# A table set that holds both ln and exp, loaded by hand ahead of the root pairs of a two-block transformer kernel

## The reference, cut to what matters

```python
def rmsnorm(t, g):
    y = t32 * lax.rsqrt(jnp.mean(t32 * t32, axis=-1, keepdims=True) + EPS)
# first block, per layer: q, k, v, gates, ... = (rmsnorm(x) * (1 + sc1) + sh1) @ w_in
#   mLSTM over chunks of 128 tokens in both directions; its gates use log_sigmoid
#   mlstm_post: h * rsqrt(mean(h * h) + EPS) per head, times sigmoid(o)
#   conv branch and gated branch, each with a layernorm; then @ w_out; x = x + g1 * ...
#   x = x + g2 * swiglu(rmsnorm(x) * (1 + sc2) + sh2)
# after both layers: rmsnorm(x, final_g)
# second block, layer 0: dilated window attention; layer 1: grouped window attention
#   x = layer_norm(ALPHA * x + h); x = x + sigmoid(x @ w_ple_gate) * (p @ w_ple_proj)
```

## Time and profile before

| | |
|---|---|
| Time, median of 3 runs | 2807.26 us (2797.67 to 2810.21) |
| The profiled execution: its time | 2797.02 us |
| The profiled execution: its span | 2795.2 us |
| Mean granted TensorE clock | 0.97 of full speed |
| HBM traffic | 86 GB/s over the span |

### The profile page before, as it was taken

How to read it: one execution, slowest core, us unless ns; L and a number is a source line. 1 busy time by engine, 2 the same in 40 slices (tenths; PEclk the granted TensorE clock), 3 DMA queues, 4 the chain that set the end, 5 groups by cost and what they waited for, 6 DMA issues and landing times.

```text
span 2795.2 us, 39634 instructions
## 1 busy us (share of the span) xinstructions
PE 2653.1 (95%) x14364; PEld 2196.1 (79%) x14364; DVE 1439.5 (51%) x2110; ACT 777.0 (28%) x1591; POOL 1614.2 (58%) x1684
## 2 busy tenths in 40 slices
PE   7799998999999997999889999899999999889998
PEld 7688887888888886788767878677888888667876
DVE  6894354564464665915543333533444444555754
ACT  3322353211121114134421111312222222233423
POOL 6343224376576664534467777676666666655464
PEclk9898999899999999999999999999999999999999
DMA  7211015133233322211123222333323333223231
GB/s 311 98 54 38 31 31 203 62 124 123 70 137 102 112 90 60 67 53 53 54 75 92 96 90 94 103 113 96 93 90 92 98 99 91 83 67 88 79 98 61
DMA packets 79406, 256.59 MB, mean 92 GB/s; under 512 B 9888, under 2 KB 13728, under 8 KB 78880
## 3 DMA queue, kind: packets, MB, share of 16 engines
q1 hardware_dynamic: 61424, 211.64, 23.3%
q10 hardware_dynamic: 17840, 43.03, 4.8%
HBM read 237.33 MB, written 2.10 MB: 86 GB/s over the span
## 4 chain that ended last, share of the span: by engine, by line
PE 44%; POOL 28%; issue 19%; DVE 5%; ACT 2%; POOLq 1%; DMA 1%; SPq 0%; ACTq 0%; DVEq 0%
POOL w_lo L421 16%; POOL w_hi L419 10%; PE PS L427 8%; PE PS L430 8%; PE PS L428 8%; PE PS L1518 4%; PE PS L1519 4%; PE PS L1520 4%; POOL word L414 2%; PE PS L1383 1%; PE PS L1401 1%; DVE Z L2208 1%; PE PS L1505 1%; DVE AC L2290 1%; DVE XL L2215 1%
## 5 line engine op out<-in xcount | busy, mean ns | idle before, releaser
L421 POOL TENSOR_TENSOR w_lo<-raw,w_hi 128x512 fp32r<-128x512 f32 (+1 forms) x662 | 951.4, 1437 | 55.3
L427 PE MATMUL PS<-XH,w_hi 128*128 128x512 f32 x2168 | 824.8, 380 | 35.0 <-DVE XL L2565 7.9
L428 PE MATMUL PS<-XL,w_hi 128*128 128x512 f32 x2168 | 796.7, 375 | 0.0
L430 PE MATMUL PS<-XH,w_lo 128*128 128x512 f32 x2168 | 747.5, 376 | 0.0
L414 POOL TENSOR_TENSOR word<-ones 128x1 f32<-128x1 f32 x331 | 93.7, 283 | 1089.1 <-PE PS L430 736.2
L419 POOL TENSOR_SCALAR w_hi<-raw 128x512 fp32r<-128x512 f32 (+1 forms) x662 | 541.7, 818 | 0.0
L427 PEld LDWEIGHTS PS<-XH,w_hi 128*128 128x128 f32 x2168 | 412.7, 190 | 144.6 <-issue 25.6
L428 PEld LDWEIGHTS PS<-XL,w_hi 128*128 128x128 f32 x2168 | 412.8, 190 | 75.6
L430 PEld LDWEIGHTS PS<-XH,w_lo 128*128 128x128 f32 x2168 | 382.6, 190 | 60.3
L1518 PE MATMUL PS<-XH,w_hi 128*128 128x512 f32 (+1 forms) x640 | 236.5, 369 | 16.0 <-DVE XL L2215 16.0
L1519 PE MATMUL PS<-XL,w_hi 128*128 128x512 f32 (+1 forms) x640 | 230.2, 360 | 0.0
(11 more groups left out here) (326 smaller groups left out, 3479.3 us busy)
## 6 DMA issues: line engine op xcount, KB each, us to landing
raw<-in_wgu SPq DMA_DIRECT2D x88, 512.0 KB, 3.5
raw<-in_wa SPq DMA_DIRECT2D x80, 512.0 KB, 3.6
raw<-in_win SPq DMA_DIRECT2D x48, 512.0 KB, 3.5
modv<-in_wmod ACTq DMA_DIRECT2D x48, 512.0 KB, 5.2
raw<-in_wdn SPq DMA_DIRECT2D x32, 512.0 KB, 3.5
QS<-Z ACTq DMA_DIRECT2D x100, 128.0 KB, 3.5
modt<-in_wmod SPq DMA_DIRECT2D x20, 512.0 KB, 15.0
raw<-in_wout SPq DMA_DIRECT2D x16, 512.0 KB, 3.5
```

Source lines behind the costliest of these rows:

```text
L421: pool.tensor_tensor(lo, src, hi.bitcast(FP32), ALU.subtract).then_inc(s_split, 1)
L427: pe.matmul(acc(s)[:, a:b], hi, rh[:, i, a:b], start=i == 0, stop=False)
L428: pe.matmul(acc(s)[:, a:b], hi, rl[:, i, a:b], start=False, stop=False)
L430: last = pe.matmul(acc(s)[:, a:b], lo, rh[:, i, a:b], start=False, stop=i == k - 1)
```

## The change

It is called at the head of `norm`, of norm 4 and of both layer norms, ahead of their waits; behind the Tanh of the third input tile, ahead of the gates' log sigmoid; and at t = 9 of the mLSTM's steps, behind the two `upper` calls. `norm` also gets a `preload_act_table(ACT.Tanh)` behind its last upper part, ahead of its last wait. No arithmetic is changed.

```diff
-        def second_act(act, link, rstd, evacuate):
+        def second_act(act, link, roots, rstd, evacuate):
...
             def layer_norm(l):
+                roots()
                 act.wait_ge(s_lsum, l + 1)
...
+            roots()
             act.wait_ge(s_squ, 5)
             rstd(TH[:, 0:SEQ], PS[:, 6, :], 1.0 / D).then_inc(s_rstd, 1)
...
+            def roots():
+                act.preload_act_table_set("natural_log_exp_and_others")
+
             def norm(q, l, w):
 
+                roots()
                 act.wait_ge(s_squ, q + 1)
...
                     last.then_inc(s_xh, 1)
+                act.preload_act_table(ACT.Tanh)
                 act.wait_ge(s_xl, KT * (q + 1))
...
                 in_tile(2, Z[:, 2], ACT.Tanh, 0.5)
+                roots()
                 act.wait_ge(s_gtm, l + 1)
...
                     if t == 9:
                         upper(0, Ug[:, 0, 0:w])
                         upper(1, Ug[:, 1, 0:w])
+                        roots()
...
-            second_act(act, link, rstd, evacuate)
+            second_act(act, link, roots, rstd, evacuate)
```

## The result

| | before | changed |
|---|---|---|
| Median | 2798.09 us, 8 runs (2793.39 to 2810.21) | 2784.36 us, 8 runs (2774.71 to 2787.27) |
| Profiled execution: time, span | 2797.02, 2795.2 us | 2785.76, 2784.0 us |
| Mean granted TensorE clock | 0.969 | 0.968 |

The ratio is 0.9935, with a 95% interval of 0.9917 to 0.9953: 18 us less (13 to 23). It is not the ratio of the two medians, which is 0.9951: the medians differ by 13.7 us, the two profiled spans by 11.2. The forecast was 15.8 us less, and 2791.5 us. From the median of before as it is measured here, 2791.5 is only 6.6 us less, about half of the 13.7 us. What a measurement can tell is about 0.5%, and 0.65% lies beyond it.

A forecast was written before the change was run, and what follows sets the result against it. PE, busy 95% of the span, bounds the kernel; only its idle time ending on table loads can be won. 6.4 + 3.3 + 4.2 - 0.1 + 2.0 = 15.8 us, so 2807.3 becomes 2791.5 us, range 2782 to 2801.

The forecast's parts named there:

- The table loads: At rstd, 4 and 4 loads left of 15 and 15; in the norms Exp starts within 0.1 us of Ln's end.
- The rival in which the load isn't counted on: The builder still puts its own loads before Ln and Exp, the new ones on top: 2811 us, chance 0.05.
- The five norms: Norms 2, 3, 4 and both layer norms each lose the 1.28 us load before Exp: 6.4 us.
- Norm 0 and the gates: Worth 0: DVE is held by POOL's instruction at norm 0, and by its own taps at the gates.
- Norm 1's 0: Worth 0: behind norm 1's Exp, PE is busy with the mod sums that DVE waits for.
- The heads, layer 0: Heads' norm in layer 0: loads go and PE's waits at the transposes shrink, 3.3 us, bounds 2.4 and 4.7.
- The heads, layer 1: Heads' norm in layer 1: PE's 3.35 us wait and 0.9 of slow transposes go, 4.2 us, bounds 3.3 and 5.0.
- The moved loads: Tanh loads moved to TH in the second block, the layer norms' projections and the cb transfer stay covered: cost nothing.
- The base: Starting time 2807.3 us, the earlier median, taken over although 10 us above the profiled execution.
- The clock: Behind both heads' norms, PE may keep its clock with the waits cut: 0 to 4.5 us, taken as 2.0.
- A: Experiments' theory: the gain ahead of norm 1 shifts PE's arrival there, and that makes the slow-clock stretch long.
- B: Experiments' theory: norm 1's own earlier Exp makes the slow-clock stretch there long.

The follow-up runs named there:

- the opposite experiment: Two more table loads between Ln and Exp of every norm, layer norm and MU, against the changed kernel: median 2803.14 us against 2783.01, ratio to before 1.0010.
- the second set: The changed kernel run once more, unaltered: ratio to before 0.9930, median 2783.01 us, profiled span 2783.1 us.
- the spread sums: The changed kernel with layer 0's twelve mod sums placed elsewhere, seven of them between tiles of the out projection: ratio to before 0.9943.
- norms alone: The changed kernel without the load at step 9, in both layers: ratio to before 0.9969, span 2787.5 us.
- each layer's heads alone: Two kernels with only the load at step 9, in one layer each: ratio to before 1.0001 for layer 0, 0.9977 for layer 1.

## Why the prediction was wrong, and which of its steps held

**The table loads: right.** 4 and 4 left, `Exp` 0.03 us behind `Ln`. The rival in which the load isn't counted on is out.

**The five norms: right, 6.4 us.** Waits of 5.62, 3.71 and 1.09 us, forecast 5.6, 3.7, 1.1; and 2.57 us for two loads in the opposite experiment.

**Norm 0 and the gates: right, 0.** Undoing them moved PE by 0.1 and 0.2 us, delaying norm 0 by 2.6 us moved it by 0.25. Norm 1's 0 can't be read: the clock moves more there than the term could.

**The heads, layer 0: 3.3 forecast, 4.0 measured** (3.8 to 4.1 in eight of the nine profiles with its load, 2.5 in the ninth; none in the others). The extra came out of PE's waits between the transposes: from the first to the last of them it is 7.56 us, not 11.80, so 4.2 less. The load at step 9 delayed the squares by 0.39 us, forecast 0.44.

**The heads, layer 1: 4.2 and some of the 2.0 for the clock forecast, 6.7 measured**, 5.1 to 7.7 from kernel to kernel; three kernels without the load there show 0.5 of drift in the same rows. The wait of 3.35 us ahead of the transposes is gone in all ten profiles with the load. What differs is PE's clock: in the three with 7.7 it didn't fall at the heads, in the three with 5.1 it was at 0.50 for 6.8 us behind them, as in three profiles that kept the wait. So some 4.6 us are the wait and what hangs on it, and up to 2.6 the clock, in some executions.

**The moved loads: right.** The Tanh load in front of `TH` in the second block, and the exponent behind it:

```profile
1850.59 1.28 ACT L844 ACT_TABLE_LOAD   x1
...
1852.77 0.72 ACT L882 ACTIVATE SM<-SM,smax 128x512 f32<-128x512 f32 x1 [0.29 <-DVE smax L1078]
```

It waits 0.29 us in place of 1.70: hidden.

**The base: the step that failed.** The sum starts from 2807.3, the median of three runs, which lay 10 us above the profiled execution "for reasons that no row shows", and those 10 us were carried over. They were the luck of three runs. Over 8, 35, 21 and 25 runs before has medians of 2798.09, 2799.83, 2799.65 and 2799.38, some 1 to 3 us above that profiled execution, and for the second profiled execution of before the median lies 3 us below it. So the term of 10 us should have been about 2. From 2799.6 the same sum gives 2783.8, and from 2798.09 it gives 2782.3; the changed kernel has 2784.36 and 2783.01. The absolute forecast, 2791.5, was 7 us too high for that reason. As a difference, 15.8 lies in both intervals (13 to 23, and 13 to 27 in the second set).

**The clock: in part right at the heads, not foreseen at norm 1.** "PE may keep its clock" came true in layer 1 of the profiled execution and not in layer 0; in the changed kernel's second execution the first matmul behind the heads ran at full clock in layer 0 and not in layer 1. A wait cut to nothing doesn't ensure it. The profiled execution was forecast at a span of 2779.4 and had 2784.0. By the table the steps gave 17 us (4.0 + 6.7 + 5 x 1.27), and 6.8 were lost between 483 and 702 us. I looked at the clock only behind PE's waits, and not where PE is busy with small matmuls and slow all the same. That PE's idle time fell by just the 15.8 us of the forecast is luck: in the forecast 2.0 of them were clock, and in the pair of second executions it fell by 17.6 (141.9 to 124.3).

**What stays open.** Of 13 profiled executions without the spread sums, six lost 10.2 to 11.9 us at norm 1 (before twice, norms alone, each layer's heads alone, the two more loads) and seven 18.8 to 23.9. The gain at the heads of layer 0 is on both sides of this, and so is norm 1's earlier `Exp`: A and B are out. That the length differs from execution to execution is shown by the two pairs with the same instructions up to there, 11.9 and 18.8 us, 10.2 and 20.4. What picks one length or the other isn't shown, nor whether the change makes the long one more likely: two profiles of before were both short, and three of the changed code up to there all long. The runs speak against a loss of 8 us in every execution: the changed kernel's fastest took 2774.7 and 2775.3 us, about 10 less than its two profiled ones, and its mean granted clock, over 15 runs, is 0.972, against 0.970 over 81 of before (the gains at the heads may be a part of that).

## What to carry to other kernels

Where two functions of different table sets follow each other on a path on which the bounding engine waits, one load of a set with both, placed ahead of the wait, is worth the load's own time and no more; count only the places where that engine really waits. A load by hand runs where it stands in the stream: behind a wait it is on the path, and nothing is won. To forecast a few per mille, forecast the difference first, and don't take over an offset of a three-run median that no row explains.

## What the runs showed of the hardware

PE's granted clock falls to 0.50 while PE is busy without a gap, in and behind chains of 32 to 48 matmuls of two columns: in every one of the 14 profiles at norm 1, in eleven of the 13 with the sums in their old places once more at the chain of 32 behind it, for 3.4 to 6.8 us, and behind three of four chains of 32 where the sums were spread. What that costs at norm 1 differs by up to 14 us between the profiles (10.2 to 23.9), about as much as the whole change gains, and it differs between executions of the same instructions. Over a whole execution the clock took 55 to 68 us by the sum above, in all kernels alike, so one profiled pair can differ by several us with no cause in the edit; a comparison instruction by instruction finds the place.

A table load on ACT takes 1283 ns and adds nothing beside that on the path: 1.31 us from `Ln` to `Exp` with one load, 2.60 with two, 0.03 with none.
